# The start and the end of a decoder trunk in smaller pieces, attention heads re-ordered, and forget-gate logits with 127 weight columns

## What is computed

```python
def fox_attention(q, k, v, f_logit):          # 8 heads of 128, layer 0
    c = jnp.cumsum(jax.nn.log_sigmoid(f_logit), axis=1)
    s = q @ k.T * d ** -0.5 + c_i - c_j       # causal
    return jax.nn.softmax(s) @ v

def cross_attention(xn, memn, wq, wkv, wo):   # 4 heads of 128, both layers
    q = xn @ wq; k, v = split(memn @ wkv)
    return softmax(q @ k.T * 128 ** -0.5) @ v @ wo

def reference(x, mem, ...):
    memn = rmsnorm(mem, norm_mem)
    h = x
    for layer in range(2):
        h = h + mixer(rmsnorm(h, norm_mix[layer]))        # layer 0: fox and retention heads
        h = h + cross_attention(rmsnorm(h, norm_xattn[layer]), memn, ...)
        h = h + square(relu(rmsnorm(h, norm_mlp[layer]) @ w1)) @ w2
    return rmsnorm(h, norm_final)
```

## Time and profile before

| | |
|---|---|
| median of 3 runs | 2455.51 us (2455.38 to 2456.51) |
| profiled execution | 2457.35 us |
| span of its instructions | 2455.2 us |
| PE busy | 2414.5 us, 98% |
| DVE, ACT, POOL busy | 60%, 49%, 14% |

### The profile page before, as it was taken

One profiled execution on the slowest core, in us unless ns is written; L12 is line 12 of the kernel. 1 busy time (PEld: TensorE's weight loads), 2 busy tenths in 40 slices (PEclk: granted clock), 3 DMA queues, 4 the chain that ended last, 5 costly groups with the idle time before them and its releaser, 6 DMA issues.

```text
span 2455.2 us, 32236 instructions
## 1 busy us (share of the span) xinstructions
PE 2414.5 (98%) x12665; PEld 2036.1 (83%) x12665; DVE 1469.2 (60%) x1786; ACT 1200.6 (49%) x1597; POOL 331.9 (14%) x442
## 2 busy tenths in 40 slices
PE   8999999999999999999999999999999999999997
PEld 7888887788888888888888877788888888888886
DVE  5546554556656556878756556566655555555555
ACT  6544455445544444544545444555645444444444
POOL 0033220010467000434310100000000000000000
PEclk9999999999999999999999999999999999999999
DMA  8555564464555566666685779864565555566563
GB/s 299 198 180 176 185 205 166 150 201 141 182 189 191 189 193 199 208 214 209 216 272 187 209 234 243 254 222 138 192 194 193 192 188 188 188 189 193 191 195 104
DMA packets 322866, 482.27 MB, mean 196 GB/s; under 512 B 18020, under 2 KB 165028, under 8 KB 322628
## 3 DMA queue, kind: packets, MB, share of 16 engines
q1 hardware_dynamic: 303860, 453.35, 56.9%
q0 software_dynamic: 4464, 15.40, 2.1%
q10 hardware_dynamic: 14432, 12.00, 1.7%
HBM read 464.51 MB, written 20.39 MB: 197 GB/s over the span
## 4 chain that ended last, share of the span: by engine, by line
PE 95%; DVE 3%; ACT 1%; DMA 1%; issue 1%; SPq 0%; DVEq 0%; ACTq 0%
PE acc L540 20%; PE acc L542 20%; PE acc L541 20%; PE acc L948 18%; PE acc L951 9%; PE at L593 2%; PE tp L569 2%; DVE wlo L1666 1%; PE at L920 1%; PE acc L920 1%; PE tp L593 1%; PE acc L831 1%; PE acc L829 1%; PE acc L830 1%; ACT whi L1127 0%
## 5 line engine op out<-in xcount | busy, mean ns | idle before, releaser
L1666 DVE TENSOR_TENSOR wlo<-raw,whi 128x1024 fp32r<-128x1024 f32 x824 | 1039.7, 1265 | 857.4 <-ACT whi L1127 854.9
L1127 ACT ACTIVATE whi<-raw 128x1024 fp32r<-128x1024 f32 x824 | 871.5, 1061 | 958.6 <-PE acc L542 613.0
L540 PE MATMUL acc<-whi,yt_hi 128*128 128x512 f32 x1472 | 578.6, 393 | 5.2 <-DVE yt_lo L1831 4.2
L542 PE MATMUL acc<-whi,yt_lo 128*128 128x512 f32 x1472 | 573.9, 390 | 0.0
L541 PE MATMUL acc<-wlo,yt_hi 128*128 128x512 f32 x1472 | 573.8, 390 | 0.0
L948 PE MATMUL acc<-x,whi 128*128 128x512 f32 x1920 | 481.3, 392 | 0.0
L948 PEld LDWEIGHTS acc<-x,whi 128*128 128x128 f32 x1920 | 346.0, 189 | 64.0 <-issue 1.6
L540 PEld LDWEIGHTS acc<-whi,yt_hi 128*128 128x128 f32 x1472 | 277.0, 188 | 64.7 <-issue 6.3
L542 PEld LDWEIGHTS acc<-whi,yt_lo 128*128 128x128 f32 x1472 | 276.8, 188 | 58.2
L541 PEld LDWEIGHTS acc<-wlo,yt_hi 128*128 128x128 f32 x1472 | 277.0, 188 | 55.7
L540 PE MATMUL acc<-whi,x 128*128 128x512 f32 x736 | 293.1, 398 | 3.6 <-DVE wlo L1666 3.6
(11 more groups left out here) (219 smaller groups left out, 1451.5 us busy)
## 6 DMA issues: line engine op xcount, KB each, us to landing
raw<-in_mlp_w SPq DMA_DIRECT2D x256, 1024.0 KB, 5.4
raw<-in_ab_w_in SPq DMA_DIRECT2D x56, 1024.0 KB, 4.9
raw<-in_cd_w_in SPq DMA_DIRECT2D x32, 1024.0 KB, 6.0
raw<-in_xa_wkv SPq DMA_DIRECT2D x16, 1024.0 KB, 6.7
raw<-in_ab_w_out SPq DMA_DIRECT2D x16, 1024.0 KB, 5.1
raw<-in_cd_w_out SPq DMA_DIRECT2D x16, 1024.0 KB, 6.6
raw<-in_xa_wq SPq DMA_DIRECT2D x8, 1024.0 KB, 5.1
ca_d<-arena ACTq DMA_DIRECT2D x16, 288.0 KB, 2.9
```

What stands on the lines that cost most here:

```text
L540: pe.matmul(a, xh, whi[:, w, kk], start=opens and kk == 0, stop=False)
L542: last = pe.matmul(a, xl, whi[:, w, kk], start=False, stop=closes and kk == 1)
L1127: act.activation(split_weights(whi, kind, i), half_weights(raw, kind, i), ACT.Copy)\
L1666: dve.tensor_tensor(split_weights(wlo, kind, i), half_weights(raw, kind, i), split_weights(whi, kind, i).bitcast(F32), ALU.subtract).then_ ...
```

## The change

The kernel's first and last pieces are made smaller. The first `mem` block and first slab are loaded in two halves each, with semaphores of their own, ahead of the gains; only block 0 is transposed ahead of the first unit. At the end, the second half of the last unit runs row tile 0 first, then row tile 1, and add, norm, scaling and output follow by row tile. Query heads are finished in the order of `Q_ORDER`, with loads of 128 columns. Fox steps stand later on PE, ACT and DVE, with `lo_head` ahead of the softmax. A half waits for each k tile's token ahead of that tile's own matmuls. The forget logits use 127 weight columns.

```diff
+Q_ORDER = [(0, 0), (1, 0), (2, 0), (0, 1), (1, 1), (2, 1), (3, 0), (3, 1)]
+Q_DONE = [Q_ORDER.index((hh, 1)) + 1 for hh in range(4)]
@@ sync: load()
+                    if kind == "query":
+                        sp.wait_ge(lo_ready, p.at("half", 2 * i + 2 - 8))
+                        for e, (hh, kh) in enumerate(Q_ORDER[2 * i:2 * i + 2]):
+                            sp.dma_start(half_weights(raw, kind, 2 * i + e),
+                                         w[kh * 1024:(kh + 1) * 1024, hh * P:(hh + 1) * P]
+                                         .rearrange("(k p) n -> p k n", p=P)).then_inc(raw_landed[i], 16)
@@ sync: start (the gains' loads now stand behind slab 1)
+            for e in range(2):
+                sp.dma_start(memt[:, :, e * L:(e + 1) * L], mem[0].rearrange("(t p) n -> p t n", p=P)[
+                    :, :, e * L:(e + 1) * L]).then_inc(mem_in[0] if e else mem_first, 16)
+                sp.dma_start(raw[:, 0, 2 * e:2 * e + 2], xa_wkv[0][e * L:(e + 1) * L, 0:NB]
+                             .rearrange("(k p) n -> p k n", p=P)).then_inc(raw_landed[0] if e else raw_first, 16)
@@ tensor: unit()
-                    for kt in (kt0, kt0 + 1):
-                        if kt in tok:
-                            wait_tp_read(pe, tok.pop(kt))
                     pe.wait_ge(lo_ready, p.at("half", i + 1))
                     for kk in range(2):
+                        if kt0 + kk in tok:
+                            wait_tp_read(pe, tok.pop(kt0 + kk))
@@ tensor: new final_pair(): halves 0 to 3 as before, then
+                for i in range(4, 8):
+                    pe.wait_ge(lo_ready, p.at("half", i + 1))
+                    last = half(i, 0)
+                    if i % 2:
+                        last.then_inc(tail_done, 1)
+                for i in range(4, 8):
+                    half(i, 1).then_inc(half_used, 1)
@@ tensor: first unit
-                    if u == 0 and i in (0, 2):
-                        mem_block(2 + i // 2)
+                    if u == 0 and i in (0, 2, 4):
+                        mem_block(1 + i // 2)
+                    if u == 0 and i == 1:
+                        gain_rows()
@@ tensor: forget_logits()
+                    m = P - 1
+                    o = bank[0:m, 0:L]
+                    wh, wl = (v[:, kt, 0:m] for v in wffs)
@@ tensor: fox_steps()
-                elif i == 1:
+                elif i == 2:
                     turn(0)
                     fox_scores(g, 2)
-                elif i == 2:
+                elif i == 3:
                     wait_freed(pe, p, 1)
                     fox_out(0, turned[0], 4 * g)
                     turn(1)
                     fox_scores(g, 3)
-                elif i == 3:
+                elif i == 4:
                     fox_out(1, turned[1], 4 * g + 1)
                     turn(2)
-                elif i == 4:
-                    turn(3)
                 elif i == 5:
                     fox_out(2, turned[2], 4 * g + 2)
+                    turn(3)
@@ tensor: queries_after() and the mixed unit's after()
-                    if i == 5:
+                    if i == 4:
                         scores(0)
-                    if i == 6:
+                    if i == 5:
                         scores(1)
                         turn(0)
-                    if i == 7:
+                    if i == 6:
                         scores(2)
                         head_out(0)
                         turn(1)
+                    if i == 7:
+                        head_out(1)
                         scores(3)
-                        head_out(1)
+                        turn(2)
                     if i == 0:
-                        turn(2)
+                        head_out(2)
                         turn(3)
                     if i == 1:
-                        head_out(2)
                         head_out(3)
@@ scalar: fox_slots()
+                elif i == 7:
+                    hi_head(4 * g)
+                    copy_turned(1, L + P)
                     softmax_exp(True, 1.0)
                 elif i == 8:
+                    hi_head(4 * g + 1)
+                    copy_turned(2, L + P)
+                elif i == 9:
+                    hi_head(4 * g + 2)
                     copy_turned(3, L + P)
                     hi_head(4 * g + 3)
@@ scalar: query slots 6 and 7, then the mixed unit's slots
+                    if i == 6:
+                        copy_query(0)
+                        act.activation(warm[:, layer:layer + 1], ident[:, 0:1], ACT.Exp)
                     if i == 7:
+                        copy_query(1)
+                        softmax_exp(False, row=9 + layer)
                     if i == 0:
                         copy_query(2)
                         softmax_exp(False, row=9 + layer)
                         copy_turned(0, 2 * L)
+                    if i == 1:
+                        hi_head(0)
+                        softmax_exp(False, row=9 + layer)
+                        copy_turned(1, 2 * L)
+                    if i == 2:
                         copy_query(3)
                         hi_head(1)
+                        copy_turned(2, 2 * L)
                         softmax_exp(False, row=9 + layer)
@@ vector: fox_slots() (slot 8: head 1, slot 9: heads 2 and 3)
                 if 4 <= i <= 7:
+                    if i == 7:
+                        lo_head(4 * g)
                     softmax_max(True, 1.0)
                     softmax_norm(True)
@@ vector: end (ACT squares, takes the root, scales and writes the left half of row tile t in the same order)
+            for t in range(TOK):
+                for n in (2, 3):
+                    dve.wait_ge(*((half_used, p.at("half", 2 * n - 6)) if t else (tail_done, n - 1)))
+                    dve.scalar_tensor_tensor(out=hb, in0=acc[:, 2 * par_ + t, :], scalar=rstd[:, 14, t:t + 1], in1=hb,
+                                             op0=ALU.mult, op1=ALU.add).then_inc(tail_add, 1)
...
+                dve.scalar_tensor_tensor(out=fin[:, t, D // 2:D], in0=h[:, t, D // 2:D], scalar=rstd[:, 7, t:t + 1],
+                                         in1=gfin[:, D // 2:D], op0=ALU.mult, op1=ALU.mult).then_inc(fin_ready, 1)
```

More of the change, by code:

```diff
@@ L356, in half_weights @@
         def half_weights(t, kind, i):
-            if kind == "heads":
+            if kind in ("heads", "query"):
                 return t[:, i // 2].rearrange("p a n -> p (a n)").rearrange("p (k h n) -> p h k n", k=8, h=2)[:, i % 2]
@@ L456, in _ @@
                 load("full", ab_w_out[0], [n * NB], order=OUT_ORDER)
-            load("heads", xa_wq[0], [0])
+            load("query", xa_wq[0], [0])
             load("mixed", xa_wo[0], [n * NB for n in range(4)])
@@ L505, in _ @@
             load("pair", cd_w_out[0], [2 * NB, 3 * NB])
-            load("heads", xa_wq[1], [0])
+            load("query", xa_wq[1], [0])
             load("mixed", xa_wo[1], [n * NB for n in range(4)])
             mlp(1)
[L510 to L513, removed]
+            for t in range(TOK):
+                sp.wait_ge(fin_ready, t + 1)
+                sp.dma_start(out[0][t * P:(t + 1) * P, D // 2:D], fin[:, t, D // 2:D]).then_inc(out_done, 16)
             sp.wait_ge(out_done, 16 * BLOCKS)
@@ L993, in last_after @@
                             h_block(1, 1)
-                    unit("pair", yt, y_tok, last_after if last and not final else u_after(3))
+                    if last and final:
+                        final_pair(y_tok)
+                    else:
+                        unit("pair", yt, y_tok, last_after if last else u_after(3))
                 step(True, False, params)
@@ L1119, in split @@
             def split(i, kind):
-                if i % 2 == 0:
-                    loads = p.bump(f"slab{i // 2}", 2 if kind == "mixed" and i < 4 else 1)
+                if p.n["unit"] == 0 and i == 0:
+                    act.wait_ge(raw_first, 16)
+                elif i % 2 == 0 or (p.n["unit"] == 0 and i == 1):
+                    loads = p.bump(f"slab{i // 2}", 2 if kind == "query" or kind == "mixed" and i < 4 else 1)
                     act.wait_ge(raw_landed[i // 2], loads * 16)
@@ L1146, in scaled, with hi_parts @@
                 last.then_inc(acc_free[par], 1)
-            def hi_parts(dst, kt0, row=None):
-                for b in range(2):
+            def hi_parts(dst, kt0, row=None, banks=(0, 1)):
+                for b in banks:
                     act.wait_ge(tp_full, p.at("tp", 1))
@@ L1264, in slot @@
                     if i == 7:
+                        if u == 0:
+                            for b in range(2):
+                                act.wait_ge(tp_free[b], gains_put[b])
                         hi_parts(xt, 4 * u, MIX)
@@ L1672, in unit, with lo_parts @@
                 p.bump("block", UNIT_BLOCKS[kind])
-            def lo_parts(dst, kt0, row=None, src=None):
-                for b in range(2):
+            def lo_parts(dst, kt0, row=None, src=None, banks=(0, 1)):
```

(11 more changed lines are left out.)

291 lines of the change are left out of this document (167 added, 124 removed).

## The result

| | before | after |
|---|---|---|
| median (lowest to highest) | 2456.01 us (2455.38 to 2457.2, 4 runs) | 2439.64 us (2438.82 to 2440.47, 4 runs) |
| profiled execution, its span | 2457.35, 2455.2 | 2440.47, 2438.5 |

What follows compares the result with a forecast made beforehand. PE's stream and its waits were taken as the bound, with 13 us of waits and 27 us of edges. Gains of 3.1 + 0.5 + 4.3 + 2.7 + 4.0 = 14.6 take 2455.5 to 2440.9 us; range 2436.5 to 2448.0.

Steps and rivals of the forecast that it cites:

- Start: Kernel start: smaller, sooner loads bring the first weight matmul 4.2 us sooner, moved transposes give back 1.1: 3.1 us gained.
- rival (c): Kernel start: first packets are slow whatever their size, so only 1.3 us gained there, 2442.7 us in all; chance 0.12.
- as long behind the first matmul as now: Kernel start: PE's clock rises from 1.2 to 2.4 GHz equally long behind the first matmul, so nothing changes.
- Rival (d): First unit: early PE pauses keep the clock low, 96 matmuls cost 19 us more, 2460 us; chance 0.03.
- Forget logits: 48 matmuls of 256 columns: with 127 weight columns the step falls from 0.120 towards 0.107 us; 0.5 us gained.
- Rival (b): Forget logits: 127 columns put each load in front of the stream, 8.6 us lost, 2450.0 at worst; chance 0.07.
- Fox heads: Two fox groups: PE lagging one half more leaves 1.6 us of waits per group instead of 3.2; 4.3 us gained.
- My walk through the two queues: Fox heads: following ACT and DVE put PE's waits at outputs 1 and 2 at 0.8 and 0.75 us.
- Rival (a): Fox heads and attention: the order only shifts waits; fox gains 1.1 us, attention nothing, 2446.8 us; chance 0.20.
- Cross-attention: Two layers: low parts of heads 1 and 3 covered, 1.5 us lost a layer instead of 2.8; 2.7 us gained.
- End: Behind the last matmul: only row tile 1 is left, tail 9.2 us instead of 13.2; 4.0 us gained.
- Sum: Whole kernel: 3.1 + 0.5 + 4.3 + 2.7 + 4.0 = 14.6 us gained, giving 2440.9 us.

Runs made afterwards that it cites:

- e2_whole_loads: Changed kernel with the first mem block and the first slab each loaded whole again, gains still behind: 2443.16 us.
- e1_cols: Changed kernel with the forget logits loading 128, 127, 64 and 8 weight columns in turn, 12 matmuls each: 2439.35 us.
- e6_fox_splits_sooner: Changed kernel with the splits of fox heads 0 and 1 one slot sooner on ACT and DVE, behind the softmax: 2436.13 us.
- e4_fox_before: Changed kernel with the fox heads' steps on PE, ACT and DVE in the order of before: 2444.02 us.
- e5_tokens_before: Changed kernel, but a half of a plain unit waits for both k tiles' tokens ahead of its first matmul: 2446.86 us.
- e11_tokens_again: Changed kernel with both k tiles' tokens waited for ahead of a plain unit's half, run again on another chip: 2443.22 us.
- e3_tail_only: Changed kernel with the last unit's matmuls in the order of before; norm, scaling and output still by row tile: 2442.91 us.
- e9_query_one_sooner: Changed kernel with fox splits, the wide unit's add, the attention's softmax 0 and query 1's copy all sooner: 2435.63 us, ratio 0.9913 to before.

## Why the prediction was right, point by point

**Start: right.** 4.2 sooner at the first weight matmul predicted, 4.5 measured; 1.1 given back predicted, 1.8 measured; in all 3.1 and 2.7. `e2_whole_loads` refutes rival (c): size matters, and more than the 0.7 us I took from the rate, as the whole block comes 1.9 us behind where its half does. That the landing came near its forecast (5.2, measured 4.94) is partly luck. I let the whole block keep its 4.7 from issue to landing, and issued at 1.19 it takes 5.6; that miss of 0.9 and the one on the size, 1.2 the other way, nearly cancel. Of the 1.8 given back, 0.8 is the transposes that now stand behind half 4 and 0.35 the gains' (read from the distance of the starts before and behind them); 0.4 is lost in the first half, to the clock, and 0.3 isn't assigned.

**Clock: the step "as long behind the first matmul as now" holds within the spread of the runs.** Steps of 0.43 us end at 17.9 in the trace before and at 14.2 in the one after, 4.0 and 4.8 behind the first weight matmul. 0.8 longer at steps of 0.43 instead of 0.23 loses 0.8 x (1 - 0.23 / 0.43) = 0.4. But the second trace of the changed kernel has them end at 13.5, 4.0 behind, and the other kernels whose first weight matmul starts at 9.0 to 9.5 have 11.7 to 14.3. So the 0.4 belongs to the profiled run and not to the change. (The clock column of the windows shows 1.00 in this stretch; the low level is read from the steps.) Rival (d) is out: it needed 73 more matmuls at the low level, and the trace after has 10 steps of 0.43 where the one before has 8.

**Forget logits: wrong by its 0.5.** The step that failed is that a wholly hidden load would give 0.107 a matmul. The step is 0.120 with 127 and with 128 columns, and still 0.116 with 8. Rival (b) is out too: no load went in front of the stream. By the rule of the Trainium skill that was weighed there ("TensorE: Matmul & The Clock Gate", "Weight-path perf modes"), only loads of 128 columns of a type other than FP32 are fast; the rows of `e1_cols`, 191 ns for 128 columns and 187 for 127, show no such difference for fp32r.

**Fox heads: mechanism right, size short.** 4.3 predicted, 5.7 measured. The new waits stand where they were put, behind low parts 0 and 1, but lose 0.5 each instead of 0.8 and 0.75: 2.0 in place of 3.1, which is 1.1 of the 1.4 us. My walk through the two queues was off by 0.3 there; `e6_fox_splits_sooner` gives the 2.1 back, so no other wait hid behind them. Rival (a) is out by `e4_fox_before`: the order alone is worth 4.5 us.

**Cross-attention: mechanism right for the low parts, wrong for the rest.** 2.7 predicted, 3.9 measured. The low parts are covered, and `e5_tokens_before` and `e11_tokens_again` show by what: with both tokens ahead of the half, head 3's wait is back in both layers (1.2 each), so the k tile's own token covered it; of head 1's only 0.2 is back, so the new order covered that. The waits that I expected in their place, 0.9 for the copy behind turn 1 and 0.6 for scores 3, are 0.3 at most beyond the step of the rows before it: my walk was off there, and why is open. In their place layer 1 alone waits 0.84 at turn 0, which I had not foreseen. The layers differ in what goes before. Layer 0's query unit begins with one block's transposes, layer 1's with two, the second behind half 1. Layer 1, PE and ACT, then layer 0, ACT:

```profile
1668.65 1.04 PE L628 MATMUL tp<-ident,h 128*128 128x128 f32 x8
...
1678.38 1.04 ACT L1199 ACTIVATE whi<-raw 128x1024 fp32r<-128x1024 f32 x1
```

```profile
558.00 1.28 ACT L1512 ACT_TABLE_LOAD   x1
...
559.41 1.04 ACT L1199 ACTIVATE whi<-raw 128x1024 fp32r<-128x1024 f32 x1
```

The first matmul of the query unit starts at 1662.04 and at 545.03. Behind the second block come the squares and the root of the norm, so the root stands on ACT 13.5 us behind the unit's start in layer 1 (1675.54) and 9.8 in layer 0, and the split of half 7 stands 16.3 behind it (1678.38) and 14.4 in layer 0. PE, which only has the transposes more, reaches turn 0 0.9 later. The 1.1 between 2.0 and 0.9 is about the wait. The two table loads of 1.28 on ACT stand in both layers, at the same places of the queue; they lengthen it, but they don't make the layers differ. No run moved the block or took the loads away, so this is read from the queues, not shown. I followed the queues for one layer and took the other as equal.

**End: right.** 4.0 predicted, 4.5 measured; `e3_tail_only` gives 3.1 of it to the order of the matmuls. The 4.6 from issue to the end were 4.4; at 371 GB/s, 1 MB of the output takes 2.8 and not the 2.7 that I took, which makes 4.5.

**Sum.** The misses go the same way at three places (1.4, 1.2, 0.5) and the other way at two (0.4, 0.5). Together they are the 2.1 by which the span's 16.7 exceed the 14.6 predicted, within rounding. So 3.1 us were missed one way and 0.9 the other: that the sum came this near is in part luck.

## What to carry to other kernels

A hand-written order pays where a wait is moved behind work of the waiting engine that doesn't need the result: here one half more of slack in the fox heads (4.5 us), and a token waited for at its own k tile (about 4 us for a moved line). Every move can show the next wait in the queue it is moved into, so follow each engine's queue for every layer by itself: here one block of transposes more made the attention's queue in layer 1 two microseconds later on ACT and 0.9 on PE. At the edges, look at what must be whole before anything starts, and at what is left when the last product ends: half loads gave 2.8 us and a row tile finished early 3.1, with no less work done.

## What the runs showed of the hardware

- PE's step for fp32r matmuls of 256 columns is 0.120 us with 128 or 127 weight columns and 0.114 to 0.116 with 64 or 8, although the load goes from 191 ns with 128 columns to 134 with 64 and 88 with 8.
- In one of thirteen traces, a wait of 1.54 us in the middle of the stream was followed by 3.4 us at the granted clock of 0.51, for a loss of about 1.6 us; the same kernel elsewhere had a wait of 0.7 and no drop, and a wait of 1.3 in `e9_query_one_sooner` and 1.2 in the kernel before had none. One case doesn't show a cause.
- The wait for `uc_d` at one and the same place goes from none in the list (`e1_cols`, `e6_fox_splits_sooner`) to 1.5 us, and the steps of 0.43 us at the start end 2.7 to 4.9 us behind the first weight matmul. For the two traces of the changed kernel, whose spans are 1.1 us apart, the wait makes 0.9 and the steps 0.3 (less 0.1 for a later first matmul).
